# Group 0 of a hybrid encoder layer on one core: the order of its first loads and of its small set-up steps, and six weight slots for it instead of three

## What is computed

```
z  = rmsnorm(x) @ w_in          # attn q,k,v | hgrn f,i,q,out-gate | gate_a | gate_b
oa = softmax(q k^T * scale + rel_bias[clip(distance)]) v       # 8 heads, own chunk + 8 past chunks of 64
fg = lb + (1 - lb) * sigmoid(f);  lb = softmax over the rows of lb_logits
ob = hgrn2(silu(q_b), 1 - fg, i, log(fg))                      # 4 heads, chunkwise recurrence
x  = x + (sigmoid(gate_a) * (oa @ w_a) + sigmoid(gate_b) * (norm(ob) * silu(g) @ w_b)) @ w_out
x  = x + PEER(rmsnorm(x))       # queries @ sub_keys, top 16 x 16 -> 16 experts per head, gather rows of u and v
y  = rmsnorm(x)
```

## Time and profile before

| | |
|---|---|
| median of three runs | 3797.7 us (3796.08 to 3798.84) |
| profiled execution, its own time | 3802.48 us |
| its span in the trace | 3800.7 us |
| TensorE busy in the span | 82% |
| VectorE busy | 71% |
| GpSimd busy | 59% |
| ScalarE busy | 23% |
| moved by DMA | 1409.65 MB, 371 GB/s on average |

### The profile page before, as it was taken

The page is one execution under the profiler, slowest core; times in us unless marked ns, Lnnn a source line. Parts: engine busy times, 40 slices in busy tenths (PEclk is TensorE's granted clock), DMA queues, the critical chain, the costliest instruction groups (busy, mean ns, idle before and its releaser), DMA issues.

```text
span 3800.7 us, 35321 instructions
## 1 busy us (share of the span) xinstructions
PE 3110.5 (82%) x11076; PEld 1832.4 (48%) x11076; DVE 2685.5 (71%) x5855; ACT 873.0 (23%) x2072; POOL 2233.9 (59%) x2224
## 2 busy tenths in 40 slices
PE   5787988897788999897799998986888898875555
PEld 4565755553356545552467455532565455321112
DVE  0335668679967696699686786799685764897775
ACT  2112222122222221222241221222231312221101
POOL 0012444576766575666665675667674754777775
PEclk8887899999899999999989999998999999998768
DMA  6478888999999999999999999999999999999998
GB/s 183 155 261 279 290 304 299 382 404 397 383 393 400 398 406 404 408 406 371 396 389 396 393 407 404 407 398 377 396 397 401 410 401 369 396 410 409 410 409 337
DMA packets 443263, 1409.65 MB, mean 371 GB/s; under 512 B 46528, under 2 KB 48064, under 8 KB 442312
## 3 DMA queue, kind: packets, MB, share of 16 engines
q0 software_dynamic: 316960, 1152.82, 78.0%
q1 hardware_dynamic: 101520, 201.08, 14.5%
q10 hardware_dynamic: 24600, 53.51, 4.0%
HBM read 1389.91 MB, written 19.95 MB: 371 GB/s over the span
## 4 chain that ended last, share of the span: by engine, by line
PE 36%; DMA 22%; DVE 18%; POOL 12%; issue 9%; ACT 2%; ACTq 0%; DVEq 0%; POOLq 0%
PE PS L668 16%; POOL ring L648 11%; DMA ring<-in_peer_v,idx 11%; PE PS L975 9%; DMA wring<-in_w_in 7%; DVE ring L1734 6%; PE PS L672 5%; DMA ring<-in_peer_u,idx 2%; PE PS L865 1%; PE PS L762 1%; PE PS L787 1%; DVE arena L1436 1%; DVE arena L1441 1%; DMA wring<-in_peer_query 1%; DVE acc L1745 1%
## 5 line engine op out<-in xcount | busy, mean ns | idle before, releaser
L975 PE MATMUL PS<-ring,diag 128*128 128x512 f32 (+1 forms) x3032 | 1550.9, 645 | 426.2 <-DMA ring<-in_peer_v,idx 394.5
L1734 DVE CUSTOM_DVE_ANT_0 ring<-ring,PS 128x1024 f32<-128x1024 f32 x1088 | 1311.9, 1212 | 274.7 <-DMA ring<-in_peer_u,idx 266.5
L648 POOL DMA_INDIRECT ring<-in_peer_u,idx x1088 | 1103.5, 1014 | 680.1 <-PE PS L975 306.2
L648 POOL DMA_INDIRECT ring<-in_peer_v,idx x1088 | 1110.0, 1020 | 620.5 <-DVE hid L1734 330.0
L975 PEld LDWEIGHTS PS<-ring,diag 128*128 128x128 f32 (+1 forms) x3032 | 556.9, 198 | 1212.6 <-issue 949.6
L668 PE MATMUL PS<-xnT,wring 128*128 128x256 f32 (+2 forms) x3840 | 768.0, 359 | 58.8 <-DMA wring<-in_w_in 39.4
L668 PEld LDWEIGHTS PS<-xnT,wring 128*128 128x128 f32 x3840 | 677.0, 199 | 177.9 <-issue 49.4
L1745 DVE SCALAR_TENSOR_TENSOR acc<-ring,wk,acc 128x1024 f32<-128x1024 f32 x330 | 424.5, 1286 | 67.6 <-issue 39.5
L1341 ACT ACTIVATE diag<-masks,wk 128x128 f32<-128x128 f32 x704 | 260.7, 396 | 675.0 <-PE PS L975 524.9
L672 PE MATMUL PS<-wring,xnT 128*128 128x512 f32 (+1 forms) x432 | 191.7, 596 | 10.0 <-DMA wring<-in_w_in 9.8
L1532 DVE SCALAR_TENSOR_TENSOR arena<-PS,arena 128x256 f32<-128x256 f32 (+4 forms) x72 | 47.8, 664 | 144.9 <-PE PS L762 94.2
(11 more groups left out here) (218 smaller groups left out, 2485.4 us busy)
## 6 DMA issues: line engine op xcount, KB each, us to landing
wring<-in_w_in SPq DMA_DIRECT2D x110, 1024.0 KB, 11.9
wring<-in_peer_query SPq DMA_DIRECT2D x40, 1024.0 KB, 12.1
wring<-in_w_out SPq DMA_DIRECT2D x20, 1024.0 KB, 11.7
ring<-in_peer_u,idx POOLq DMA_INDIRECT x1088, 13.7
ring<-in_peer_v,idx POOLq DMA_INDIRECT x1088, 13.9
arena<-rel_scr ACTq DMA_DIRECT2D x80, 144.0 KB, 6.3
wring<-in_w_branch_a SPq DMA_DIRECT2D x10, 1024.0 KB, 16.4
wring<-in_w_branch_b SPq DMA_DIRECT2D x10, 1024.0 KB, 14.5
```

The costliest lines, as they stand in the source:

```text
L648: pool.indirect_dma_start(ring[:, SLOT[n], :], None, u_tab if kind == "u" else v_tab, bass.IndirectOffsetOnAxis(ap=idx[:, at:at + 1], axis ...
L975: mm = pe.matmul(PS[0:rows, 6 + half, :], diag[:, seq % ND, 0:rows], ring[:, SLOT[n], 512 * half:512 * (half + 1)], start=(seq == pe_of[tn ...
L1734: dve.tensor_tensor_reduce(row, row, xp_row, 1.0, 0.0, ALU.mult, ALU.add, hid[:, m % 2, k:k + 1]).then_inc(dve_used, 1)
```

## The change

It concerns group 0 alone.

- `rel_bias` is loaded as it lies (8 rows of 513) into `rel_raw`, as ACT's first load; DVE turns it into `rel` with a copy that reads backwards, and fills the lower half right after.
- The `lb_logits` load has its own semaphore, and the subtraction, the sigmoid and `one_lb` stand at the start of stage D. The square of x waits for x and for the memset of `ss`.
- Weights of group 0 up to w_out use six slots: three in `wring`, three in `ring` (its slots 4 to 9). `weight_slots` makes the list: which slot, which turn of it, and which block was there before.
- The sub-keys are loaded after six blocks instead of three, into `ring`. They are turned in stage F, four blocks in each head of the recurrence, into the PSUM banks 6 and 7, and copied by ACT to `ring`. ACT writes them to DRAM at the end of the fourth head.
- ACT loads the bias tables of heads 0 and 1 before it copies v from PSUM (before: after it).

```diff
+def weight_slots(n, early):
+    last, uses = [-1] * NWE, [0] * NWE
+    slot, turn, before = [], [], []
+    for b in range(n):
+        s = min(range(NWE if b < early else NW), key=lambda x: (last[x], x))
...
             def load_weights(b):
-                if b >= NW:
-                    sp.wait_ge(pj_ready, last_product[b - NW] + 1)
+                if block_before[b] is not None:
+                    sp.wait_ge(pj_ready, last_product[block_before[b]] + 1)
...
-                if b == NW - 1:
+                if b == NWE - 1:
                     sp.dma_start(sk, sub_keys[0]...).then_inc(sk_in, 16)
...
+                        if g == 0:                       # PE, in each head h of the recurrence
+                            if h == 0:
+                                pe.wait_ge(sk_in, 16)
+                            if h >= 2:
+                                pe.wait_ge(sk_cp, h - 1)
+                            for k in range(4):
+                                mm = pe.transpose(PS[:, 6 + h % 2, k * P:(k + 1) * P], sk[:, 4 * h + k, :], ident[:, :])
+                            mm.then_inc(sk_tr, 1)
...
+                act.dma_start(rel_raw, rel_bias[0]).then_inc(rel_in, 16)
                 act.dma_start(gain_mix[:, :], ...).then_inc(const_in, 16)
-                act.dma_start(lbl[:, :, :], ...).then_inc(const_in, 16)
-                act.dma_start(rel[:, 383:767], bass.AP(rel_bias.tensor, NREL - 1, [[NREL, HA], [-1, 384]])).then_inc(rel_in, 16)
+                act.dma_start(lbl[:, :, :], ...).then_inc(lb_in, 16)
-            act.wait_ge(lb_d, 1)
-            act.activation(lb[:, :], lbl[:, 0, :], ACT.Sigmoid).then_inc(lb_a, 1)
...
+                    if g == 0 and what == "v":
+                        act.wait_ge(rel_out, 16)
+                        load_bias(g, 0)
+                        load_bias(g, 1)
...
                     if ti == nt - 1:                     # ACT, end of stage F: as before
                         if g == 0:
                             act.wait_ge(sk_out, 16)
                         act.dma_start(skT, sk_scr).then_inc(skT_in, 16)
...
-            dve.wait_ge(const_in, 32)
-            dve.tensor_tensor(lbl[:, 0, :], lbl[:, 0, :], lbl[:, 1, :], ALU.subtract).then_inc(lb_d, 1)
-            dve.wait_ge(lb_a, 1)
+            dve.wait_ge(rel_in, 16)
+            dve.tensor_copy(rel[:, 383:767], rel_raw[:, NREL - 1:NREL - 385:-1])
+            dve.tensor_copy(rel[:, 0:383], rel_raw[:, NREL - 1:NREL].to_broadcast([HA, 383])).then_inc(relE, 1)
```

More of the change, by code:

```diff
@@ L45 @@
 NW = 3
+NWE = 6
 R = 15
@@ L304, in plan_projections @@
     return blocks, sets, products, parts
+def weight_slots(n, early):
[3 more added lines that the diff above has]
+        s = min(range(NWE if b < early else NW), key=lambda x: (last[x], x))
+        slot.append(s)
+        turn.append(uses[s])
+        before.append(last[s] if uses[s] else None)
+        uses[s] += 1
+        last[s] = b
+    return slot, turn, before
 def build(nc, x_prompt, x_sample, cache_k, cache_v, state_in, norm_mix, w_in, rel_bias, lb_logits,
@@ L312, in build @@
     blocks, sets, products, parts = plan_projections()
+    early = sum(len(mine) for mine, _, _, first, _ in sets if products[first][0] == 0 and products[first][1] != "I")
+    block_slot, block_turn, block_before = weight_slots(len(blocks), early)
     last_product = {}
@@ L462, in build, with weight_block @@
         held = ring[:, HELD + 2:HELD + 4, :].rearrange("p a b -> p (a b)")
+        def weight_block(b):
+            n = block_slot[b]
+            if n < NW:
+                return wring[:, n, :].rearrange("p (k n) -> p k n", k=4)
+            return ring[:, 2 * n - 2:2 * n, :].rearrange("p a b -> p (a b)").rearrange("p (k n) -> p k n", k=4)
         def in_held(at, *shape):
@@ L480, in build @@
         rel = arena[0:HA, 12 * WG:12 * WG + 767]
-        sk = cut(arena[:, 0:2048], 16, P)
-        skTs = part(3072, 16, P)
+        rel_raw = arena[0:HA, 16 * WG:16 * WG + NREL]
+        sk = cut(ring[:, 0:2, :].rearrange("p a b -> p (a b)"), 16, P)
+        skTs = cut(ring[:, 2:4, :].rearrange("p a b -> p (a b)"), 16, P)
+        lb_in, ss_set = sem("lb_in"), sem("ss_set")
         const_in, rel_in, sk_in, relE, rel_out, sk_tr, sk_cp, sk_out, consts, lb_d, lb_a, state_loaded = [
@@ L489, in build @@
         merged = sem("merged")
-        w_in_sem = [sem(f"w_landed{n}") for n in range(NW)]
+        w_in_sem = [sem(f"w_landed{n}") for n in range(NWE)]
         pj_ready = sem("pj_ready")
@@ L725, in mix @@
                         mm.then_inc(kt_tr, 1)
[L726 to L731, removed]
                 yield
@@ L1054, in mix @@
                 yield
+                if g == 0:
+                    act.wait_ge(const_in, 16)
                 for ti, (tid, rows, c0) in enumerate(tiles):
@@ L1107, in mix @@
                 act.dma_start(gain_hgrn, bass.AP(hgrn_norm.tensor, 0, [[0, P], [1, DA]])).then_inc(gh_in, 16)
[L1108 to L1117, removed]
                 yield
@@ L1176, in mix @@
                        .then_inc(oT_cp, 1)
+                if g == 0:
+                    act.wait_ge(lb_d, 1)
+                    act.activation(lb[:, :], lbl[:, 0, :], ACT.Sigmoid).then_inc(lb_a, 1)
                 yield
                 yield from sigmoid_gates(g, "D", W)
-                if g == 0:
-                    act.wait_ge(sk_out, 16)
                 if any(k_tiles[q] for q in range(g + 1)):
@@ L1240, in mix @@
                             outputs(h - 1)
+                        if g == 0:
+                            act.wait_ge(sk_tr, h + 1)
+                            act.activation(skTs[:, 4 * h:4 * h + 4, :], PS[:, 6 + h % 2, :].rearrange("p (a b) -> p a b", a=4),
+                                           ACT.Copy).then_inc(sk_cp, 1)
                         yield
@@ L1245, in mix @@
                     outputs(HB - 1)
+                    if g == 0:
+                        act.wait_ge(sk_cp, 4)
+                        act.dma_start(sk_scr, skTs.rearrange("p a b -> p (a b)")).then_inc(sk_out, 16)
                     if tid == SAMPLE:
@@ L1561, in mix @@
                     dve.wait_ge(kv_out, 32 * sum(len(k_tiles[q]) for q in range(g + 1)))
+                if g == 0:
+                    dve.wait_ge(lb_in, 16)
+                    dve.tensor_tensor(lbl[:, 0, :], lbl[:, 0, :], lbl[:, 1, :], ALU.subtract).then_inc(lb_d, 1)
+                    dve.wait_ge(lb_a, 1)
+                    link(dve.tensor_scalar(one_lb[:, :], lb[:, :], -1.0, 1.0, ALU.mult, ALU.add))
                 yield
```

22 lines of the change are left out of this document (7 added, 15 removed).

## The result

The changed kernel takes 3775.4 us (median of 4 runs, 3772.8 to 3777.9) against 3798.3 us for the kernel before (4 runs, 3796.1 to 3803.0). The ratio is 0.9936, with a 95% interval of 0.9924 to 0.9948: 22.9 us, 0.6%, faster. Forecast were 3769 and a range of 3757 to 3782. The profiled execution took 3772.8 us, with a span of 3771.0.

What follows compares the result with a forecast made beforehand. A nearly full DMA stream bounds the kernel from the first gather on; group 0's lead passes on one to one. Terms 25.7 + 3.7 - 0.3 = 29.1 us took the median 3797.7 to 3769 us, range 3757 to 3782.

Steps and rivals of the forecast that it cites:

- The start: Opening of group 0: the square no longer waits behind lb and starts at 6.0 instead of 14.22, 8.2 us earlier.
- q, k, v: First products of group 0: waits for weights go, v ends at 37.9, a gain of 10.1 us.
- The case of even sharing: Loads during q, k, v: bias table and weights share bandwidth evenly, block 5 lands near 31, in time, 0 lost.
- Sub-keys and the first table: Before attention: sub-key work leaves, 4.8 us gone; first bias table earlier, 2.6 us; first add at 40.3.
- rival 2: Before attention: ACT is held by a late bias table copy, slower by over 0.2% beyond 59 us; chance 0.03.
- Rest of attention: Group 0, first add to D: stays at 22.9 us, bounds 18.1 and 32.4, so D starts at 63.2.
- rival 1: Attention: early weight blocks crowd the bias tables, two more delayed pairs of heads cost 9.6 us, 3778; chance 0.15.
- lb at D: Start of stage D: computing lb there costs 0, under 2 us without cover.
- Six slots: Stages D to H: three more products' lead removes the weight waits of E and H, 3.7 us gained.
- Recurrence: Stage F: turning sub-keys hides in PE's idle time; issuing the sk_scr load loses 0.3 us.
- rival 3: Recurrence in stage F: added PE work raises its clock to full level, 6.1 us gained, 3763; chance 0.07.
- rival 4: After the first gather: the stream loses what the start gained, 3797 or so; chance 0.05.

Runs made afterwards that it cites:

- The hold experiments: Changed kernel with weight blocks from 8, or from 6, held until the seventh head's add, and sub-keys loaded after block 11: 3767.8 and 3762.3 us.
- the norm alone: Kernel before, with only the norm of x moved ahead of the lower bound lb: 3791.1 us, one execution.
- the best version: Changed kernel with blocks from 6 held until the seventh head's add, sub-keys after block 11, norm's gain loaded ahead of the raw bias: 3760.7 us, ratio 0.9905.
- the line alone: Kernel before, with only the bias line changed: raw bias loaded first and turned by copies on VectorE: 3798.5 us, one execution.
- the first experiment: Changed kernel with weight blocks from 8 held until the seventh head's add and sub-keys loaded after block 11: 3767.8 us, ratio 0.9919.

## Why the prediction was right, and where it was off

*The start (8.2 us).* Right: the square at 5.9 (forecast 6.0). The raw line landed by 2.6 us, far inside the bound of 12.0. The gain cost 0.9 us of the 0 to 1.1 that were left open; I had taken 0.

*q, k, v (10.1).* Right: v at 37.9 as forecast, 0.9 us late in q and about as much won back behind it. The case of even sharing held, though barely: it had block 5 near 31, and it landed at 34.1, 0.95 us after PE came to it.

*Sub-keys and the first table (4.8 and 2.6).* Right: the tables issued at 32.3 (forecast 31.0), first add at 39.64 (40.3). ACT stood 1.3 us for the table, and no one waited for it; the copy took 23.0 us, where rival 2 needed 51, so that one did not come about.

*Rest of attention, kept at 22.9 us.* This step failed. It took 32.0, just under the upper bound of 32.4, which is rival 1. My argument against it was the total: 53 us of transfers fit ahead of 63. But from the third head on a table is asked for only when the head two before it has been read, and has to be there a few microseconds later; what else fills the DMA engines in just that time decides, not the sum. The hold experiments take the blocks out of that time and leave all bytes in place, and attention falls to 19.6 us. The estimate of 61.5 for D's earliest start, worked out from a limit that the Trainium skill states (DMA: Bandwidth & Descriptors, Specifications), never came to bind: the changed kernel's D is at 71.63, with idle DMA engines ahead of it, and a stretch above ran at 390 GB/s, over that limit of 358.

The Trainium skill (DMA: Bandwidth & Descriptors, Queues, rings and completion order) says that a DMA engine takes turns between the queues that have work, a packet at a time. The landings agree: in the first 80 us a table on ACT's queue took 6.5 us beside weight blocks that themselves took 21.8 (median, those for `ring`), longer than the 2.8 it needs with the blocks held, and not behind all of them.

*lb at D (0).* Right: D's first products run on without it.

*Six slots (3.7).* Right for E and H, where no weight wait is left; and D and E together took 57.9 us instead of 62.3, 2.3 more of a gain than E's term of 2.0. D's first 64 records took 9.42 us instead of 10.28 (0.9), the 128 records ahead of E's products of L698 14.3 instead of 15.3 (1.0), and the rest, up to the table load ahead of F, 14.55 instead of 16.9 (2.4). The first of these is luck: PE's granted clock was 0.77 on average in those records and 0.70 before, and no part of the change aims at it. The others hold E's 1.99 and shorter waits for weights, of 0.16 to 0.35 us before, that the sum had put at nothing.

*Recurrence (0.3 lost).* It took 44.6 us instead of 44.9, so nothing was lost. The four rows of L900 took 0.7 to 1.1 us each, PE still idled about 2 us for DVE in each head, and 12 records of L883 took 2.7 to 2.9 us. The granted clock was a little higher, 0.61 on average from F's exponential to its output where it was 0.58, but of the 6.1 us of rival 3 at most these 0.3 came.

*Sum.* Against the forecast the first gather is 5.5 us late (243.74 for 238.2): -0.7 at the first add, +9.1 in attention, -2.3 in D and E, -0.6 in the recurrence; G, H and the queries gave 1.6 where 1.7 was expected. So rival 1 came in almost full, at 9.1 of its 9.6 us, and the time lies below the 3778 it was given because other terms won 3.6 us that were not forecast, some of them by luck. The range held because it had been drawn to contain this rival. From the first gather on the lead is kept. The median minus the first gather is 3531.0 us before, 3531.7 after, and 3530.4 to 3534.3 in the four other kernels that were timed: rival 4 is out.

## What to carry to other kernels

More buffers let loads run earlier, and early bytes are not free: they compete with whatever small load is on the path at that time. Look not only at whether the bytes fit ahead of a deadline but at which loads are asked for late and needed at once, and hold the others until those are issued; here one wait on SP and a later place for one load were worth another 10 us or so (0.9908 for 0.9936), close to half of what the change gave. And parts of a change whose waits hide one another cannot be priced alone: three of them summed to 9 us alone and to 18.8 together, with three slots and with the first tables asked for earlier, which was not run alone.

## What the runs showed of the hardware that was not expected

- A load of 1024 pieces of 4 bytes (`gain_mix`) landed in 4.4 to 4.6 us as its queue's first load (before, the norm alone, the best version) and in 10.7 to 11.1 as its second, behind the raw line of 16 KB, with three slots (the line alone, the change with three slots) and with six (changed, held) alike. The logits, 1024 pieces too, took 11.0 to 11.2 as second behind the gain and 21.0 to 23.2 as third behind both in that order, but 11.8 as third when the gain had gone first. So the raw line is dear where it goes first and not where it goes second, and the three more weight blocks on SP's queue make no difference; why, no run here shows.
- Issuing itself can hold a queue's engine: SP spent 13.65 us on two blocks at 21.66, 12.1 of them on the first, and 8.73 on two at 36.23. The same two blocks took 0.37 each at 21.79 and 23.58 without the sub-keys ahead of them (first experiment), and 0.92 together at 52.08 with the blocks held. The DMA engines were half idle for part of that time (0.51 from 25 to 30 us); what in the sub-keys' load does it, no run here shows.
